# Sums of squares of five norms placed inside the next projection's contraction

## What is computed

```
y = x * rsqrt(mean(x * x) + 1e-6) * g
proj = y @ w
```

## Time and profile before

| | us |
|---|---|
| three runs, median (lowest to highest) | 1689.82 (1688.92 to 1689.87) |
| the profiled execution, its own time | 1687.73 |
| its span, first to last instruction | 1685.9 |
| PE busy with matmuls in the span | 1591.5 |
| DVE busy | 754.7 |
| ACT busy | 563.0 |
| mean granted PE clock | 0.976 of full |

### The profile page before, as it was taken

One profiled execution on the slowest core, in us unless ns is written; L12 is line 12 of the kernel. 1 busy time (PEld: TensorE's weight loads), 2 busy tenths in 40 slices (PEclk: granted clock), 3 DMA queues, 4 the chain that ended last, 5 costly groups with the idle time before them and its releaser, 6 DMA issues.

```text
span 1685.9 us, 23691 instructions
## 1 busy us (share of the span) xinstructions
PE 1591.5 (94%) x10153; PEld 1256.4 (75%) x10155; DVE 754.7 (45%) x1092; ACT 563.0 (33%) x686; POOL 2.9 (0%) x8
## 2 busy tenths in 40 slices
PE   7998999889999999999889999999999999999998
PEld 6696889644544444444478888999998888899997
DVE  2555633421111111111287774666547675566643
ACT  2462422311110101111253743444333484344431
POOL 0000000000000000000000000000000000000000
PEclk9997999989999999999989999999999999999999
DMA  6642228259999999999544224556542431555640
GB/s 223 217 154 100 80 96 325 100 198 400 422 422 422 422 422 422 422 422 422 208 150 147 103 100 149 169 182 220 205 167 84 171 130 51 200 172 179 225 150 26
DMA packets 129784, 374.20 MB, mean 222 GB/s; under 512 B 9271, under 2 KB 54631, under 8 KB 105127
## 3 DMA queue, kind: packets, MB, share of 16 engines
q1 hardware_dynamic: 125735, 370.71, 57.7%
q0 software_dynamic: 528, 2.04, 0.4%
q10 hardware_dynamic: 3440, 0.25, 0.2%
HBM read 371.92 MB, written 1.06 MB: 221 GB/s over the span
## 4 chain that ended last, share of the span: by engine, by line
PE 75%; DVE 9%; DMA 9%; ACT 4%; issue 2%; ACTq 1%; SPq 0%; DVEq 0%
PE bank L577 31%; PE bank L922 10%; DMA ring<-in_w_exp_up 7%; PE bank L1091 7%; PE bank L601 4%; PE bank L943 4%; DVE parts L1525 3%; PE bank L795 2%; PE bank L898 2%; PE bank L906 2%; PE bank L623 2%; PE bank L555 2%; DMA ring<-in_w_out 1%; ACT parts L1188 1%; PE bank L923 1%
## 5 line engine op out<-in xcount | busy, mean ns | idle before, releaser
L577 PE MATMUL bank<-hnr,parts 128*128 128x256 f32 x4032 | 486.6, 281 | 0.0
L577 PEld LDWEIGHTS bank<-hnr,parts 128*128 128x128 f32 x4032 | 479.7, 189 | 5.1 <-issue 4.8
L1525 DVE TENSOR_TENSOR parts<-ring,parts 128x2048 fp32r<-128x2048 f32 x136 | 306.2, 2287 | 129.2 <-ACT parts L1188 128.8
L1188 ACT ACTIVATE parts<-ring 128x2048 fp32r<-128x2048 f32 x136 | 252.9, 1902 | 164.2 <-DMA ring<-in_w_out 59.2
L922 PE MATMUL bank<-ring,G 128*64 128x512 f32 x512 | 223.7, 592 | 3.0 <-DMA ring<-in_w_exp_up 1.9
L923 PE MATMUL bank<-ring,G 128*64 128x512 f32 x512 | 223.9, 593 | 0.0
L922 PEld LDWEIGHTS bank<-ring,G 128*64 128x64 f32 x512 | 69.5, 137 | 136.3 <-issue 136.1
L577 PE MATMUL bank<-SKr,parts 128*128 128x256 f32 x960 | 123.5, 291 | 12.2 <-DVE SKr L1691 10.3
L577 PEld LDWEIGHTS bank<-SKr,parts 128*128 128x128 f32 x960 | 120.8, 199 | 15.2 <-issue 9.7
L943 PE MATMUL bank<-ring,SZ 128*64 128x512 f32 x256 | 112.8, 593 | 9.8 <-ACT SZ L1324 9.8
L1091 PE MATMUL bank<-Gr,parts 128*128 128x256 f32 x640 | 115.3, 283 | 0.0
(11 more groups left out here) (297 smaller groups left out, 1590.4 us busy)
## 6 DMA issues: line engine op xcount, KB each, us to landing
ring<-in_w_exp_gate SPq DMA_DIRECT2D x64, 1024.0 KB, 13.2
ring<-in_w_exp_up SPq DMA_DIRECT2D x64, 1024.0 KB, 16.5
ring<-in_w_exp_down SPq DMA_DIRECT2D x64, 1024.0 KB, 11.1
ring<-in_w_in SPq DMA_DIRECT2D x60, 1024.0 KB, 7.3
ring<-in_w_ffn_in SPq DMA_DIRECT2D x44, 1024.0 KB, 7.7
ring<-in_w_ffn_out SPq DMA_DIRECT2D x20, 1024.0 KB, 6.0
ring<-in_w_out SPq DMA_DIRECT2D x12, 1024.0 KB, 6.5
ring<-in_w_ckv SPq DMA_DIRECT2D x4, 1024.0 KB, 13.7
```

The source lines that it names most:

```text
L577: m = mm(b(name)[:, T * half:T * half + T], part(chunk, ws)[:, k, P * mt:P * mt + P], src[xs][:, k, :], start=k == 0 and i == 0, stop=k == ...
L1188: A(parts[:, 2 * (r % 2), 2048 * i:2048 * i + 2048], ring[:, CHUNK[chunk][0], 2048 * i:2048 * i + 2048], ACT.Copy).then_inc(high_made, 1)
L1525: v.tensor_tensor(parts[:, 2 * (r % 2) + 1, at], ring[:, CHUNK[chunk][0], at], parts[:, 2 * (r % 2), at].bitcast(F32), ALU.subtract).then_ ...
```

## The change

For each of the five norms, PE now makes a first part of the next projection's contraction for all four half groups of its first chunk, then the sum of squares, and then the rest of the contraction for the same four half groups. For `cq` the first part is k = 0 to 4, for `dq.l` and `ffn0.l` it is k = 0 to 5 (new helper `split_around`). Both halves of a bank are now open at once, so only the first product of a bank carries the start flag. The bank list is reordered to match. On ACT and DVE, half 0 of the parts of `dk.0` moves ahead of the root, half 1 stays where both halves were, and the parts of `ffn1.l` move ahead of the root.

```diff
--- before.py
+++ after.py
@@ -127,14 +127,14 @@
         if h % 2 == 0:
             g += [f"mo{h // 2}"]
     g += [f"pa{i}" for i in range(4)] + [f"pb{i}" for i in range(4)] + [f"ou{i}" for i in range(4)]
-    g += ["n_cross", "cq0", "cq1"] + [f"cs{h}" for h in range(4)]
+    g += ["cq0", "cq1", "n_cross"] + [f"cs{h}" for h in range(4)]
     g += ["ct0", "ct1", "co0", "ct2", "co1", "ct3", "co2", "co3"]
     g += [f"cw{i}" for i in range(4)]
     g += ["n_moe", "routeT", "route"] + [f"ht{i}" for i in range(4)] + ["rank"]
     first = list(g)
     second = [f"at{i}" for i in range(4)] + ["n_final"]
     for l in range(LAYERS):
-        s = ["n_attn", "dq0", "dq1", "dk0", "dk1", "rq0", "rq1", "rk0", "rk1", "dv0", "dv1", "ds0", "de0",
+        s = ["dq0", "dq1", "n_attn", "dk0", "dk1", "rq0", "rq1", "rk0", "rk1", "dv0", "dv1", "ds0", "de0",
              "sq0", "sq1", "dt0", "ds1", "de1", "sk0", "sk1", "do0", "dt1", "ds2", "de2", "sv0", "sv1", "do1",
              "dt2", "ds3", "de3", "bz0", "bz1", "ga0", "do2", "dt3", "ba0", "ga1", "do3"]
         for h in range(8):
@@ -148,9 +148,8 @@
             if h % 2 == 0:
                 s += [f"bo{h // 2}"]
         s += [f"pa{i}" for i in range(4)] + [f"pb{i}" for i in range(4)] + [f"ou{i}" for i in range(4)]
-        s += ["n_ffn"]
         for j in range(11):
-            s += [f"fg{j}", f"fu{j}"]
+            s += [f"fg{j}", f"fu{j}"] + (["n_ffn"] if j == 0 else [])
         s += [f"fo{i}" for i in range(4)]
         second += [f"{n}.{l}" for n in s]
     second += ["n_last"] + [f"yt{i}" for i in range(4)]
@@ -583,6 +582,27 @@
                 for j, name in enumerate(names):
                     split_tile(chunk, src, name, 2 * j, fresh if j == 0 else None)
                     split_tile(chunk, src, name, 2 * j + 1)
+
+            def split_around(chunk, src, names, fresh, between):
+
+                for at, to in ((0, 6), (6, KT)):
+                    for name in names:
+                        if at == 0:
+                            room(pe, name)
+                        for half in range(2):
+                            mt = 2 * names.index(name) + half
+                            for k in range(at, to):
+                                ready(chunk, k)
+                                if k % 2 == 0:
+                                    pe.wait_ge(fresh[0], fresh[1] + k // 2 + 1)
+                                for i, (ws, xs) in enumerate(PASSES):
+                                    m = mm(b(name)[:, T * half:T * half + T], part(chunk, ws)[:, k, P * mt:P * mt + P],
+                                           src[xs][:, k, :], start=k == 0 and i == 0 and half == 0,
+                                           stop=k == KT - 1 and i == 2, skip_group_check=True)
+                        if to == KT:
+                            fin(m, name)
+                    if at == 0:
+                        norm_sum(between)
 
             def hn_fresh(name):
                 return hn_split, 4 * SPLIT_NORMS.index(name)
@@ -802,8 +822,22 @@
                       om, lambda: [emptied(pe, f"mo{i}") for i in range(4)], 0)
 
 
-            norm_sum("n_cross")
-            linear_f("cq", hn, ["cq0", "cq1"], h_at=16)
+            landed(pe, "cq")
+            w = wide[CHUNK["cq"][0]]
+            for at, to in ((0, 5), (5, KT)):
+                for name in ("cq0", "cq1"):
+                    if at == 0:
+                        room(pe, name)
+                    for half in range(2):
+                        mt = 2 * (name == "cq1") + half
+                        for k in range(at, to):
+                            pe.wait_ge(h_ready, 16 + k + 1)
+                            m = mm(b(name)[:, T * half:T * half + T], w[:, k, P * mt:P * mt + P], hn[:, k, :],
+                                   start=k == 0 and half == 0, stop=k == KT - 1, skip_group_check=True)
+                    if to == KT:
+                        fin(m, name)
+                if at == 0:
+                    norm_sum("n_cross")
 
             def cross_scores(h):
                 room(pe, f"cs{h}")
@@ -981,8 +1015,7 @@
 
             for l in range(LAYERS):
                 x = f".{l}"
-                norm_sum("n_attn" + x)
-                split_f("dq" + x, z_parts, ["dq0" + x, "dq1" + x], (xg_split, 4 * l))
+                split_around("dq" + x, z_parts, ["dq0" + x, "dq1" + x], (xg_split, 4 * l), "n_attn" + x)
                 split_f("dk" + x, z_parts, ["dk0" + x, "dk1" + x])
                 for name in ("dq0", "dq1", "dk0", "dk1"):
                     emptied(pe, name + x)
@@ -1074,9 +1107,9 @@
                 merge_out(x, ["proj_diff" + x, "proj_sb" + x], od, lambda: pe.wait_ge(og_ready, l + 2),
                           ob, lambda: [emptied(pe, f"bo{i}{x}") for i in range(4)], l + 1)
 
-                norm_sum("n_ffn" + x)
-                for j in range(11):
-                    split_f(f"ffn{j}{x}", hn_parts, [f"fg{j}{x}", f"fu{j}{x}"], hn_fresh("n_ffn" + x) if j == 0 else None)
+                split_around("ffn0" + x, hn_parts, ["fg0" + x, "fu0" + x], hn_fresh("n_ffn" + x), "n_ffn" + x)
+                for j in range(1, 11):
+                    split_f(f"ffn{j}{x}", hn_parts, [f"fg{j}{x}", f"fu{j}{x}"])
                 for i in range(4):
                     room(pe, f"fo{i}{x}")
                 for c in range(5):
@@ -1355,10 +1388,11 @@
                 norm_squares("n_attn" + x, xres, [f"fo{j}.{l - 1}" for j in range(4)] if l else None, xg_highs)
                 if l == 0:
                     high("dq.0", [1])
+                    high("dk.0", [0])
                 norm_root("n_attn" + x)
                 hn_highs("n_attn" + x)
                 if l == 0:
-                    high("dk.0")
+                    high("dk.0", [1])
                 if l == 0:
                     act.wait_ge(lam_sums, 1)
                     A(lam_e, lam_s, ACT.Exp).then_inc(lam_exps, 1)
@@ -1446,8 +1480,8 @@
                         high("ffn0" + x)
 
                 norm_squares("n_ffn" + x, xres, [f"ou{j}{x}" for j in range(4)], ffn_beside)
+                high("ffn1" + x)
                 norm_root("n_ffn" + x)
-                high("ffn1" + x)
                 for j in range(11):
                     emptied(act, f"fg{j}{x}")
                     A(hid_raw[j % 3], hid_raw[j % 3], ACT.Silu).then_inc(hid_silu, 1)
@@ -1913,6 +1947,7 @@
                 xg_low(l, 3)
                 if l == 0:
                     low("dq.0", [1])
+                    low("dk.0", [0])
                 emptied(dve, name)
                 link(v.reciprocal(root, root))
                 for j in range(4):
@@ -1922,7 +1957,7 @@
                 hn_low(name, 3)
                 take_scaled("dq0" + x, two(dq, 0), over_tiles(root))
                 if l == 0:
-                    low("dk.0")
+                    low("dk.0", [1])
                 take_scaled("dq1" + x, two(dq, 1), over_tiles(root))
                 low("dv" + x)
                 take_scaled("dk0" + x, two(dk, 0), over_tiles(root))
@@ -2043,9 +2078,9 @@
                         freed(v.tensor_copy(ob[:, h // 2, :], b(name)[:, 0:T]), name)
                 merge(x, l + 1)
                 hn_low("n_ffn" + x, 3)
+                low("ffn1" + x)
                 emptied(dve, "n_ffn" + x)
                 link(v.reciprocal(ffn_root, ffn_root))
-                low("ffn1" + x)
                 by_root = over_tiles(ffn_root)
                 for j in range(11):
 
```

## The result

The changed kernel takes 1709.28 us (median of 4 runs, 1706.43 to 1710.83) against 1689.37 for the kernel before in the same measurement (1685.63 to 1689.87). The ratio is 1.0114 with a 95% interval of 1.0100 to 1.0127: the change makes the kernel slower, by 17 to 21 us. The forecast was 1708.7. The profiled execution has a span of 1704.6 us against 1685.9, 18.7 us more, where the sum of the terms was 18.9.

What follows compares the result with a forecast made beforehand. PE was taken to bound the kernel, with matmuls in flight for 94% of the span. The terms 0 + 1.2 + 12.8 + 4.9 = 18.9 us, on the median of 1689.82, gave 1708.7; own range 1705 to 1712, 8-in-10 range 1700 to 1714.

Steps and rivals of the forecast that it cites:

- What there was to win: PE's waits for squares: 16.1 us over all norms, 6.3 at n_attn.0, 2.5 at n_attn.1, nothing at three of five places.
- n_cross, 0: At cq: the later sum costs nothing, as the root still comes before cq0's take, hidden by 2.6 us.
- n_ffn, +0.6 each: At n_ffn.0 and n_ffn.1: PE waits 0.6 us for the low part of pair 2 of x; later root hidden.
- n_attn.0, +12.8: Layer 0's attention norm: late root holds dk.0's half 1, 9.0 us late, plus 3.8 us for PE's clock.
- slow starts: At n_attn.0: PE starts dense work at 1.2 GHz after each of two waits, 1.9 us each.
- n_attn.1, +4.9: Layer 1's attention norm: rope 3.1 us later through the late root and dk1's take, plus 1.8 us for a clock fall.
- The rule on banks: Rival: each change of bank costs PE idle time in dq, ffn0 and cq, about 60 us more, 1768; 1%.
- the clock stays at 2.4 GHz: Rival: no clock fall in the new waits, 9.0 + 3.1 + 1.2 = 13.3 us, 1703; 17%.
- a root chain that holds nobody: Rival: takes and dk.0's half 1 don't hold PE; only dq's delay counts, 3.2, 1.5 and 1.2 us, 1696; 6%.
- The further waits: Rival: more such waits further on, or a third and fourth slow start, 5 us more, 1714; 8%.

Runs made afterwards that it cites:

- pairs kernel: Kernel before with only n_attn.1 changed: squares and products taken by pairs of tiles, the sum never put off; ratio 0.9977 to the kernel before.
- run with 960 products: Kernel before with ffn1 to ffn10 multiplied k by k, going to another bank after every 6 products; 960 products took 113.07 us, 113.06 before.
- kept-busy run: Changed kernel plus idle products in PE's two waits at n_attn.0; from n_final's reciprocal to layer 0's first rope product 49.81 us, 3.25 under the changed kernel.
- run with the split at 4: Changed kernel with the contraction split at k = 4 in place of 6 in split_around, cq unchanged; ratio 1.0067 to the kernel before.

## Why the prediction was right, step by step

- **What there was to win.** The waits of 2.5 us at n_attn.1 were real: the pairs kernel has one of 1.04 us left of them and is 2.0 us faster there. The change could not win this, since it put the sum behind pair 2 of x.
- **n_cross, 0.** Right: 8.64 + 3.45 + 5.18 = 17.27 us on the chain against 3.45 + 13.81, no new wait, and the root came before cq0.
- **n_ffn, +0.6 each.** Right: PE is idle for 0.71 us in both layers, and the stage is longer by 0.93 in layer 0 and 0.68 in layer 1.
- **n_attn.0, +12.8.** Measured 12.67. The waits: 9.0 forecast, 9.4 with the clock held up. The two slow starts: 1.9 each forecast, 1.48 and 1.78 measured (8.94 - 7.46 and 12.12 - 10.34).
- **n_attn.1, +4.9.** Measured 5.19, and 4.3 to 4.5 in the three other kernels with this order. Of the 5.19, 1.9 are the slow start (60 products in 9.39 us, against 7.46 with the clock held up at n_attn.0), forecast as 1.8 and by no means certain. The rest is 3.3, against 3.1: 1.4 are the queue on DVE ahead of dk1, and the 1.8 that stay when this is moved are PE's own, as the sum no longer lies in waits. The working puts this last share at 1.5, though its own times give 1281.2 - 1279.4 = 1.8.
- **The rule on banks.** It was given 1%, and the run with 960 products rules it out for this kernel. The micro-idle between groups that the Trainium skill (TensorE: Matmul & The Clock Gate, "A second HAM failure mode: psum-queue depth-cycling") tells of did not show here.
- **The other rivals.** That the clock stays at 2.4 GHz fell with the kept-busy run; a root chain that holds nobody fell with the wait of 6.8 us. The further waits that were named, such as sq's parts behind a later dv, did not come. There were more clock falls, but in code that the change leaves alone, and in both directions: 1.5 us less in layer 0, 1.2 and 0.9 more in layer 1.

The mechanism came out as forecast place by place. That the total is within 1 us of the median is partly luck: at n_attn.0 the waits were 0.4 us too low and the slow starts 0.5 too high, and runs of one and the same kernel lie further apart than the miss.

The same theory was less good in the run with the split at 4, where the expectation left the second slow start out. The mechanism predicted well only as long as every new wait was also priced for what follows it.

## What to carry to other kernels

Before moving a small reduction behind other work to fill waits, ask who waits for its result: here 3.45 us of sum were put off, the root came 13 us later (1.5 of them by a slow start), and an in-order engine had the next weights' parts queued behind the root. Put off the work nobody waits for, and take squares and products in the order in which their inputs come, as the pairs kernel does; that filled the waits at n_attn.1 with a gain (at n_attn.0 it was not tried). And check each new wait of a few us on PE twice, once for its length and once for the clock after it.

## What the runs showed that I had not expected

The price of a slow start did not follow the length of the wait: 84 products took 12.12 us behind 6.84 us of idling and 12.69 us behind 3.96. A wait of 2.7 us took the clock down in layer 0 before the change and not in layer 1, and the 180 products by `w_out`, which no edit touched, took from 21.83 to 24.23 us in the traces of these kernels, behind waits of 1.2 us and less. What decides whether the clock falls there is left open. Products whose result is thrown away kept the clock up and made stretch A 3.25 us shorter; as the waits themselves are what should go, that is a probe more than a remedy.
